# Loading the cached keys and values of a stream with one transfer each

## The reference

```python
def fox_block(q, k, v, fq, fk, q_pos, k_pos):
    s = jnp.einsum('bqhd,bkhd->bhqk', q, k, preferred_element_type=jnp.float32) * (HEAD_DIM ** -0.5)
    s = s + jnp.swapaxes(fq, 1, 2)[..., :, None] - jnp.swapaxes(fk, 1, 2)[..., None, :]
    mask = (k_pos[None, :] <= q_pos[:, None])[None, None]
    p = jax.nn.softmax(jnp.where(mask, s, -jnp.inf), axis=-1)
    return jnp.einsum('bhqk,bkhd->bqhd', p.astype(v.dtype), v)
...
        k_all = jnp.concatenate([past_k.astype(k.dtype), k], axis=1)
        v_all = jnp.concatenate([past_v.astype(v.dtype), v], axis=1)
        F_all = jnp.cumsum(jnp.concatenate([past_logf.astype(jnp.float32), logf], axis=1), axis=1)
        att = fox_block(q, k_all, v_all, F_all[:, P:], F_all, P + jnp.arange(T), jnp.arange(P + T))
```

## Time and profile before

| | us |
|---|---|
| median of three runs | 3522.26 |
| lowest and highest run | 3514.09, 3525.69 |
| span of the profiled execution | 3511.3 |
| stream attention in it | about 1436 to 1642 |

### The profile page before, as it was taken

One profiled execution on the slowest core, in us unless ns is written; L12 is line 12 of the kernel. 1 busy time (PEld: TensorE's weight loads), 2 busy tenths in 40 slices (PEclk: granted clock), 3 DMA queues, 4 the chain that ended last, 5 costly groups with the idle time before them and its releaser, 6 DMA issues. The chain is left out here.

```text
span 3511.3 us, 61012 instructions
## 1 busy us (share of the span) xinstructions
PE 3187.4 (91%) x22604; PEld 2932.6 (84%) x22604; DVE 1989.2 (57%) x3345; ACT 1445.7 (41%) x2433; POOL 268.0 (8%) x273
## 2 busy tenths in 40 slices
PE   4999997589999999786895999999999999999997
PEld 2999997168877788554785999999999999999997
DVE  4656663568887789443563445454445445454443
ACT  2344442068877788333232323323232322323231
POOL 0000001011111111110000000020002000020001
PEclk7999998689999999898997999999999999999999
DMA  5566565844343431696777322252223322242221
GB/s 189 200 224 239 204 226 172 283 106 118 82 117 82 116 82 35 200 327 216 201 224 234 104 84 84 86 183 87 86 90 138 131 84 84 93 176 94 85 84 38
DMA packets 350295, 499.23 MB, mean 142 GB/s; under 512 B 24944, under 2 KB 282488, under 8 KB 343481
## 3 DMA queue, kind: packets, MB, share of 16 engines
q1 hardware_dynamic: 338253, 453.81, 41.3%
q0 software_dynamic: 11904, 43.79, 3.4%
HBM read 377.14 MB, written 107.95 MB: 138 GB/s over the span
## 5 line engine op out<-in xcount | busy, mean ns | idle before, releaser
L2272 PE MATMUL c_psu<-c_hT,c_up_hi 128*128 128x272 f32 x4096 | 682.7, 289 | 29.3 <-DVE c_up_lo L2194 19.8
L2272 PEld LDWEIGHTS c_psu<-c_hT,c_up_hi 128*128 128x128 f32 x4096 | 582.8, 189 | 30.5 <-DVE c_up_lo L2194 20.2
L2214 DVE TENSOR_TENSOR c_ffT<-c_ffT,c_psd 128x544 f32<-128x544 f32 x512 | 369.4, 721 | 398.3 <-PE c_psd L2289 392.0
L2154 ACT ACTIVATE c_relu<-c_psu 128x544 f32<-128x544 f32 x128 | 80.0, 625 | 997.3 <-PE c_psu L2272 997.3
L2289 PE MATMUL c_psd<-c_a_hi,c_dn_hi 128*128 128x272 f32 x2048 | 423.7, 288 | 3.6 <-DVE c_ffT L2214 3.6
L2272 PE MATMUL c_psu<-c_hT,c_up_lo 128*128 128x272 f32 x2048 | 425.6, 289 | 0.0
L2289 PE MATMUL c_psd<-c_a_hi,c_dn_lo 128*128 128x272 f32 x2048 | 423.9, 288 | 0.0
L2289 PE MATMUL c_psd<-c_a_lo,c_dn_hi 128*128 128x272 f32 x2048 | 422.2, 288 | 0.0
L632 PE MATMUL p_psm<-p_whi,p_hT_hi 128*128 128x384 f32 (+1 forms) x952 | 323.4, 340 | 16.8 <-DVE p_wlo L525 9.9
L2289 PEld LDWEIGHTS c_psd<-c_a_hi,c_dn_hi 128*128 128x128 f32 x2048 | 322.0, 188 | 4.5 <-DVE c_ffT L2214 3.4
L2289 PEld LDWEIGHTS c_psd<-c_a_lo,c_dn_hi 128*128 128x128 f32 x2048 | 321.9, 189 | 0.0
(11 more groups left out here) (234 smaller groups left out, 5206.8 us busy)
## 6 DMA issues: line engine op xcount, KB each, us to landing
c_up_raw<-in_w_up_dram SPq DMA_DIRECT2D x64, 1024.0 KB, 5.5
c_dn_raw<-in_w_down_dram SPq DMA_DIRECT2D x64, 1024.0 KB, 4.7
p_raw<-in_w_in_dram SPq DMA_DIRECT2D x24, 1536.0 KB, 7.2
s_krows<-in_cache_k_dram SPq DMA_DIRECT2D x16, 1536.0 KB, 6.7
s_vrows<-in_cache_v_dram POOLq DMA_DIRECT2D x16, 1536.0 KB, 7.6
o_wm<-in_w_mod_dram SPq DMA_DIRECT2D x16, 1024.0 KB, 6.9
q_split<-p_split SPq DMA_DIRECT2D x34, 384.0 KB, 2.3
k_split<-p_split SPq DMA_DIRECT2D x34, 384.0 KB, 2.4
```

Of the source, the lines that this page charges most:

```text
L2154: act.activation(r[:, g, :].rearrange("p (h n) -> p h n", h=2), ps_u[g][:, :, 0:HW], ACT.Relu).then_inc(relu_done, 1)
L2214: dve.tensor_tensor(out, out, ps_d[d % 2][:, :, 0:HW], ALU.add).then_inc(dn_free, 1)
L2272: last = pe.matmul(ps_u[g][:, half, 0:HW], w[p][:, k, f], x[:, k, half * HW:(half + 1) * HW], start=(k == 0 and j == 0), stop=(k == KT - 1 ...
```

## The change

`k_rows`, `v_rows` and `v_new` become two buffers each that hold all twelve heads of a stream, twice the space. SP issues one key load of 3 MB (3072-byte runs) for a stream, after all keys of stream b-2 have been turned, and then the bias rows of both halves as before. POOL issues one value load and one load of new values for a stream, after all values of stream b-2 have been used, and then does the two mask additions, each after the bias rows of its half. PE waits for keys and values only in the first half of a stream, and takes its columns from the wider tiles. The loop body now holds two streams (so that the buffer is a constant), and three turns take the place of six. Computation, transferred bytes and the order on PE, ACT and DVE are as before.

```diff
-        k_rows = sb("s_krows", [P, 2, CT, QKV_W])
-        v_rows = sb("s_vrows", [P, 2, CT, QKV_W])
-        v_new = sb("s_vnew", [NEW, 2, QKV_W])
+        k_rows = [sb(f"s_krows{i}", [P, CT, ATT]) for i in range(2)]
+        v_rows = [sb(f"s_vrows{i}", [P, CT, ATT]) for i in range(2)]
+        v_new = [sb(f"s_vnew{i}", [NEW, ATT]) for i in range(2)]
...
-            body(0)
-            body(1)
-            with eng.Fori(2, STREAMS) as b:
-                body(b)
+            for p in range(2):
+                body(p, 0, p)
+            with eng.Fori(1, STREAMS // 2) as j:
+                for p in range(2):
+                    body(2 * j + p, j, p)
...
+                wait_past(sp, S["k_turned"], 12 * (b - 1))
+                src = t["cache_k"][0, bass.ds(b, 1), :, :, :]
+                sp.dma_start(k_rows[p][:], src.rearrange("o (n p) h d -> p (o n) (h d)", p=P)).then_inc(k_in[p], 16)
                 for s in range(2):
                     g = 2 * b + s
-                    wait_past(sp, S["k_turned"], 6 * (g - 1))
-                    src = t["cache_k"][0, bass.ds(b, 1), :, s * HG:(s + 1) * HG, :]
-                    sp.dma_start(k_rows[:, s], src.rearrange("o (n p) h d -> p (o n) (h d)", p=P)).then_inc(k_in[s], 16)
...
+                if not isinstance(b, int):
+                    pool.wait_ge(S["valued"], 2 * (b - 1))
+
+                    pool.sem_inc(S["waited_v"], 1)
+                src = t["cache_v"][0, bass.ds(b, 1), :, :, :]
+                pool.dma_start(v_rows[p][:], src.rearrange("o (n p) h d -> p (o n) (h d)", p=P)).then_inc(v_in[p], 16)
+                pool.dma_start(v_new[p][:], t["v_s"][bass.ds(b * NEW, NEW), :]).then_inc(v_in[p], 16)
                 for s in range(2):
                     g = 2 * b + s
-                    cols = slice(s * QKV_W, (s + 1) * QKV_W)
-                    if not (isinstance(b, int) and b == 0):
-                        pool.wait_ge(S["valued"], g - 1)
-
-                        pool.sem_inc(S["waited_v"], 1)
-                    src = t["cache_v"][0, bass.ds(b, 1), :, s * HG:(s + 1) * HG, :]
-                    pool.dma_start(v_rows[:, s], src.rearrange("o (n p) h d -> p (o n) (h d)", p=P)).then_inc(v_in[s], 16)
-                    pool.dma_start(v_new[:, s], t["v_s"][bass.ds(b * NEW, NEW), cols]).then_inc(v_in[s], 16)
                     pool.wait_ge(bias_in[s], 16 * HG * (b + 1))
...
-            def keys(g, b, s):
-                pe.wait_ge(k_in[s], 16 * (b + 1))
+            def keys(g, j, p, s):
+                if s == 0:
+                    pe.wait_ge(k_in[p], 16 * (j + 1))
...
-            def values(g, b, s):
-                pe.wait_ge(v_in[s], 32 * (b + 1))
+            def values(g, j, p, s):
+                if s == 0:
+                    pe.wait_ge(v_in[p], 32 * (j + 1))
```

More of the change, by code:

```diff
@@ L1480, in _, with body @@
                 sp.dma_start(mask[NEW * m:NEW * (m + 1), :], mask[0:NEW, :]).then_inc(S["mask_in"], 16)
-            def body(b):
+            def body(b, j, p):
+                wait_past(sp, S["k_turned"], 12 * (b - 1))
+                src = t["cache_k"][0, bass.ds(b, 1), :, :, :]
+                sp.dma_start(k_rows[p][:], src.rearrange("o (n p) h d -> p (o n) (h d)", p=P)).then_inc(k_in[p], 16)
                 for s in range(2):
                     g = 2 * b + s
-                    wait_past(sp, S["k_turned"], 6 * (g - 1))
-                    src = t["cache_k"][0, bass.ds(b, 1), :, s * HG:(s + 1) * HG, :]
-                    sp.dma_start(k_rows[:, s], src.rearrange("o (n p) h d -> p (o n) (h d)", p=P)).then_inc(k_in[s], 16)
                     wait_past(sp, S["least"], g - 1)
@@ L1645, in keys @@
                         last = pe.transpose(ps_k[part][:, P * i:P * i + P],
-                                            k_rows[:, s, 4 * part + i, P * a:P * a + P], ident[:])
+                                            k_rows[p][:, 4 * part + i, QKV_W * s + P * a:QKV_W * s + P * a + P], ident[:])
                     last.then_inc(S["k_turned"], 1)
@@ L1681, in values @@
                         m = P if i < CT else NEW
-                        rhs = v_rows[:, s, i, P * a:P * a + P] if i < CT else v_new[:, s, P * a:P * a + P]
+                        cols = slice(QKV_W * s + P * a, QKV_W * s + P * a + P)
+                        rhs = v_rows[p][:, i, cols] if i < CT else v_new[p][:, cols]
                         last = pe.matmul(ps_o[PR * a:PR * a + PR, 0:P], pT[0:m, i, PR * a:PR * a + PR], rhs,
@@ L1701, in _, with body @@
             pe.wait_ge(S["out0"], 4)
-            def body(b):
+            def body(b, j, p):
                 for s in range(2):
                     g = 2 * b + s
-                    keys(g, b, s)
+                    keys(g, j, p, s)
                     if not (isinstance(b, int) and b == 0):
-                        values(g - 2, b - 1, s)
+                        values(g - 2, j if p else j - 1, 1 - p, s)
                     scores(g, s)
@@ L1714, in _ @@
             groups(pe, body)
-            values(GROUPS - 2, STREAMS - 1, 0)
+            values(GROUPS - 2, STREAMS // 2 - 1, 1, 0)
             turn_out(GROUPS - 2)
             turn(GROUPS - 1, 1)
-            values(GROUPS - 1, STREAMS - 1, 1)
+            values(GROUPS - 1, STREAMS // 2 - 1, 1, 1)
             turn_out(GROUPS - 1)
```

## The result

| | before | after |
|---|---|---|
| median us, 20 runs each on one chip | 3522.38 | 3530.92 |
| lowest and highest | 3514.09, 3532.35 | 3523.85, 3537.32 |
| span of the profiled execution | 3511.3 | 3522.4 |
| ratio, 95% interval | | 1.0027 (1.0019 to 1.0034) |

The changed kernel is 8.5 us slower. The forecast was 1.0 us faster. The time lies inside the range, but the sign is wrong, and the loss lies in a stage that the change does not touch. A timed value is some 1.5 us above the span of its own execution (3523.85 and 3522.4 for the one profiled of after), so the profiled execution of before, 3511.3, is shorter than all 20 timed ones; differences between single profiles are read with that in mind. Two executions of before among those made beside the experiments took 5313 and 6351 us, in a slower state of the chip, and are left out of every median and ratio.

What follows compares the result with a forecast made beforehand. In stream attention, the prediction held that steady groups wait for GpSimd's late mask addition, not for transfers. Terms -6.4 and +5.4 sum to -1.0 us, giving 3521.3 us against the 3522.26 median, range 3511 to 3532.

Steps and rivals of the forecast that it cites:

- Step (4): Stream loop: TensorE's body grows from 161 to 319 instructions, no fetching anew expected, 0 us.
- Step (1): Stream attention: early mask additions let reductions start sooner, 0.45 us for each of groups 4 to 14, sum -6.4 us.
- the reduction does not wait for the mask addition: Rival, stream attention: the reduction waits for something unseen, so only the start counts, 3527.7 us; chance 0.10.
- a shift of the spells: TensorE's spells of lower granted clock, about every fourth group, may shift and move the time 1 or 2 us either way.
- Step (2): Start of stream stage: first keys, now 3 MB, land 6.4 us later; second and third key waits (1.0 us) go; net +5.4.
- No later wait for keys: Sign of being right, stream stage: after the first key transposes, TensorE never waits for keys again.
- The first rival: Stream stage: DMA engines become the bound once pace drops under 0.35 MB/us; 3547 us, or 3534 nearer the edge; chance 0.12.
- Step (3): Load issues: SyncE issues 8 key loads for 16, GpSimd 8 and 8 for 16 and 16; nothing more gained, 0 us.
- the fourth rival: Stream loads: fewer transfers pay by themselves, 2.8 us for each of 16 removed loads, 45 us, time 3476; chance 0.03.

Runs made afterwards that it cites:

- Loop_of_two: The kernel before with only the loop holding two streams and turning three times, loads, waits and buffers unchanged: 3535.49 against 3523.66 us, ratio 1.0028.
- pad_64: The changed kernel with 64 short semaphore instructions added at the head of TensorE's stream code: 3515.16 us, one execution.
- pad_128: The changed kernel with 128 short semaphore instructions added at the head of TensorE's stream code: 3513.88 us, one execution.
- moved_code: The changed kernel with 64 short semaphore instructions at the head of TensorE's output projection, behind the stream stage: 3518.73 against 3522.39 us, ratio 0.9985.
- before_moved_code: The kernel before with 192 short semaphore instructions at the head of TensorE's output projection: 3542.07 us, one execution.
- mask_late: moved_code with GpSimd's mask additions held until the scores of their group are done: 3531.13 against 3522.18 us for before, ratio 1.0026.
- mask_first: The kernel before with GpSimd's mask addition put ahead of its wait for values and its two loads: 3504.78 against 3523.66 us, ratio 0.9944.
- before_moved_96: The kernel before with 96 short semaphore instructions at the head of TensorE's output projection: 3536.78 us, one execution.

## Why the prediction was wrong, point by point

**Step (4), the loop, "So 0", is the step that failed.** It saw that TensorE's loop body grows from 161 to 319 instructions, and asked whether that body would be fetched anew. In the stream stage of after no stall of this kind stands, and q8 has no packet from 1540 to 1620 us. But it asked nothing of the code behind it: every later instruction of TensorE moves too. And the row that it leaned on, covers 2000 to 2200 us, inside a block, where only the inner loop turns. The outer loop of channel mixing, with 808 matrix instructions on TensorE in kernel.py (some 860 with the waits), turns back near 2315 and 2719 us, and there after has its 6 packets each. In the prediction's sum there should have stood two turns of 9.3 us, 18.6, against the 0. Loop_of_two (402.96 and 402.76 us), pad_64, pad_128 and moved_code (394.3), and before_moved_code (402.9) show it. That it would strike, and what a turn costs, could not have been read from the trace of before alone; that the code behind moves, and that two turns of a long loop stand there, could.

**Step (1), the mask addition: mechanism right, size too small.** The reduction did wait for GpSimd, and mask_late shows it. The regular group fell by 0.62 us (10.65 to 10.03), not 0.45. The reduction now starts 0.31 us behind the scores (1537.64 to 1537.95) where I took 0.41. And the exponential is not held by ScalarE's small copy as far as I took it: it starts at 1539.23, 1.82 us behind the start of the last scores, where before it was 2.45. That is 0.63 us gained, more than the 0.55 that I had put as the end, since it begins 0.07 us before the copy's record ends. The rival "the reduction does not wait for the mask addition" is refuted by mask_first and mask_late. What mask_first gains by its median (18.9 us on its chip) is more than 0.62 x 11 and 1.3 for the last group give, and more than the 8.0 us by which its profiled span is shorter. A reason is the execution that was profiled of before: its span, 3511.3, lies 11 us under the median, that of mask_first (3503.3) only 1.5 us under its own.

Two other profiles show where such 10 us can lie. Before_moved_96 and before_moved_code have the stream code of before, and their stream stages took 215.9 and 212.5 us in place of 205.6. The windows over the ten regular groups, in before, before_moved_96 and before_moved_code:

```profile
1501.61:1611.04 109.43, 88.44 (x1060) 61.36 (x1060) 45.39 (x110) 40.17 (x81) 16.77 (x30) 0.97 0.94 316
1503.27:1622.75 119.48, 99.70 (x1060) 70.54 (x1060) 45.39 (x111) 40.21 (x81) 16.83 (x30) 0.86 0.90 290
1507.05:1622.98 115.93, 95.69 (x1060) 67.27 (x1060) 45.40 (x111) 40.20 (x81) 16.80 (x30) 0.90 0.92 299
```

The same instructions take 109.4, 119.5 and 115.9 us at a granted clock of 0.97, 0.86 and 0.90; in before_moved_96 every one of these groups takes 11.7 or 12.2 us in place of 10.65. Mask_first had 0.98 there, and its stage is 19.5 and 22.9 us shorter than theirs, which is about its gain by medians. Some 7 us of that are the shorter regular groups (11 of 0.62); much of the rest may be fewer spells of low clock. That the usual execution of before looks like these two, and why mask_first has fewer spells, is not shown. The prediction let a shift of the spells be worth 1 or 2 us; by these profiles they are worth 7 to 10.

**Step (2), the first keys: right in kind, undersized, and its second half wrong.** From the issue of the first keys to the first transposes passed 17.6 us in place of 9.76, +7.8 against +6.4 (and 18.7 to 19.1 in four kernels with the same loads). The mis-sized term is the pace of the keys. The queues of after from 1448 to 1457 us:

```profile
q0 software_dynamic: 417, 2.56, 67.8%
q1 hardware_dynamic: 414, 1.27, 34.7%
```

The queues do take packets in turn, 417 and 414, as the step said, but GpSimd's packets are 6.1 KB, where the step left them at the 4.6 of the earlier trace rows, and the keys' are 3.1, so the keys get 0.14 MB/us and not 0.17. "No later wait for keys" was wrong: five of them, 5.1 us.

**The first rival, the DMA engines as the bound, is true in part.** I put its edge at 0.35 MB/us. From 1529 to 1569 us, four regular groups of after, the window reads:

```profile
1529.00:1569.00 40.00, 34.07 (x425) 23.42 (x424) 18.23 (x45) 15.77 (x32) 3.53 (x7) 1.00 1.02 335
```

The engines are busy without a gap and move 335 GB/s, 0.335 MB/us, where the prediction held this rival off with 0.40 to 0.42, while two groups of 10.03 us need 7.1 MB in 20.06 us, 0.354. By these numbers the lead of the loads melts by about 1 us a stream (an estimate), and then TensorE waits. In moved_code this can be followed: three transposes wait 1.82, 2.01 and 2.21 us for keys (1528.56, 1570.93, 1614.71), and exactly these groups take 12.1, 13.5 and 12.8 us, with a granted clock of 0.86, 0.75 and 0.87 over the group and 1.00 in those between. So a key wait of 2 us comes with a group that is 2 to 3.5 us longer. It need not be its cause: before has three such groups too (12.1, 12.2 and 13.0 us, from 1522.91, 1566.93 and 1611.04) with no key wait in them. I had given this rival 20 us where it turns decisive; it did not become that, because so few groups pass.

**Step (3), fewer issues, 0:** held; nothing in any run speaks for a gain. Nor is there a sign of the fourth rival, that fewer transfers pay by themselves: mask_late has the wide loads and is 0.26% slower. The Trainium skill, page "DMA: Bandwidth & Descriptors", section "Bandwidth", recommends transfers of at least 1 MiB; the loads of before had 1.5 MB already. The fixed cost of about 2 us, for which the prediction named that section, stands in the same page's section on the anatomy of one DMA. By these traces that cost was hidden, and what showed is the other side of large loads: TensorE waits for the whole of the first one.

**The sum.** That the time lies inside the range is luck: two large errors partly cancel. In the two profiled executions: stream stage -6.7, output projection -0.3, channel mixing +18.6 (its first block +0.2), all else -0.7 or so, together +11.1 (3522.4 against 3511.3). The forecast had -1.0, 0 and 0 for the first three. Behind the first reduction the stream stage gave 14.4 us where the sum had 7.4: the groups 4 to 14 came out near their term (5.3 against 4.95), and the rest are groups 1 to 3 (2.9 against 0.2, and 1.0 for the key waits), the last group (2.95 against 1.3) and the stretch behind it (3.3, for which the sum had no term). By medians it is +8.5. The moved code, taken out by moved_code, is 12 us by medians and 15 us by ratios, less than the 18.6 in the blocks. I lay this to the executions: the stream stage of after took 198.9 us and that of moved_code 208.7, with the same stream code, at a granted clock of 0.97 and 0.94 over the ten regular groups, and the executions profiled lie differently among their runs (after's is the shortest of its 20, moved_code's in the upper half). This difference was not followed further.

## What to carry to other kernels

A longer loop body moves all code behind it on the same engine; after any change in instruction count, look at the turns of the later loops for idle time put down to "issue" in the middle of a row of matmuls, and compare the packets of the instruction queue. Before widening a transfer, look whether something small stands behind it on its queue or engine: here the gain in each group was a mask addition that came out from behind a wait, and two statements in another order give it without the wide loads. And where a group gets shorter, check what the transfers need per group against what the engines move; 0.354 against 0.335 MB/us was the next bound, and waits for keys came with loads of either size.

## What the hardware showed that I had not expected

- The place of code alone, with equal work, changed the time by 9.3 us at each turn of a loop with 808 matrix instructions: 4.8 and 0.7 us standing, the rest in matmuls at the lower clock (1.2 GHz) for some 8 us behind it. 16 added instructions left it, 64 removed it, with 256 it was there again.
- Executions with the same stream code differ in that stage by up to 10 us: 198.9 and 208.7 us with wide loads, the shorter with two spells of low granted clock in its regular part and the longer with three, and 205.6, 212.5 and 215.9 us with the code of before, at a granted clock of 0.97, 0.90 and 0.86 over the ten regular groups. So the stage of a single profile cannot carry a difference of this size.
- A mask addition of 0.21 us on GpSimd was worth 0.4 to 0.6% of the kernel by its place in the order alone (mask_late against moved_code, mask_first against before), of which some 7 us, 0.2%, can be followed in the shorter regular groups.
